# Projections from rows that are not yet normed, in a two-layer hybrid encoder

## What is computed

```python
h = rms_norm(x, norm1_g[i])          # x * rsqrt(mean(x^2) + 1e-6) * g, per token
proj = h @ w_in[i]
q, k, v, z, xbc, dt_raw, gate_a, gate_m = jnp.split(proj, SPLITS, axis=-1)
q = rms_norm(q.reshape(b, s, 8, 2, 64), qk_norm_g[i, 0])   # per head of 64
k = rms_norm(k.reshape(b, s, 8, 2, 64), qk_norm_g[i, 1])
...
u = silu(conv(xbc, width 5, along the tokens) + conv_b)
dt = softplus(dt_raw + dt_bias);  y = y * silu(z)
```

## Time and profile before

| | us |
|---|---|
| median of three runs | 1734.61 |
| the profiled execution, its own time | 1734.33 |
| its span, first to last instruction | 1732.5 |
| TensorE busy in the span | 1686.1 |
| VectorE, ScalarE, GpSimd busy | 718.0, 683.6, 667.9 |

### The profile page before, as it was taken

How to read it: one execution, slowest core, us unless ns; L and a number is a source line. 1 busy time by engine, 2 the same in 40 slices (tenths; PEclk the granted TensorE clock), 3 DMA queues, 4 the chain that set the end, 5 groups by cost and what they waited for, 6 DMA issues and landing times.

```text
span 1732.5 us, 23236 instructions
## 1 busy us (share of the span) xinstructions
PE 1686.1 (97%) x8975; PEld 1046.0 (60%) x8975; DVE 718.0 (41%) x1351; ACT 683.6 (39%) x1549; POOL 667.9 (39%) x536
## 2 busy tenths in 40 slices
PE   8999999999999999999899999999999999999997
PEld 6889877787434444343378898777874344444342
DVE  6728788524222222221176287875242222122121
ACT  5565787754211111111156557877541111111111
POOL 7788776895000000000077987768940000000000
PEclk9999999999999999999999999999999999999999
DMA  7454312766999999999954452227589999999997
GB/s 285 184 195 152 141 50 102 284 265 275 408 428 428 427 428 427 426 428 428 424 212 162 179 195 98 84 106 283 233 320 414 427 428 427 427 428 428 426 427 311
DMA packets 44659, 528.47 MB, mean 305 GB/s; under 512 B 4824, under 2 KB 7640, under 8 KB 12288
## 3 DMA queue, kind: packets, MB, share of 16 engines
q1 hardware_dynamic: 44512, 526.89, 74.1%
q0 software_dynamic: 32, 0.02, 0.0%
HBM read 525.82 MB, written 1.06 MB: 304 GB/s over the span
## 4 chain that ended last, share of the span: by engine, by line
PE 70%; DMA 13%; DVE 9%; ACT 5%; issue 2%; POOL 1%; SPq 0%; DVEq 0%; ACTq 0%
PE PS L1286 19%; DMA view<-in_w_exp_up_dram 12%; PE PS L1317 11%; PE PS L870 8%; PE PS L872 8%; PE PS L871 8%; DVE view L1987 5%; PE PS L1232 3%; PE PS L1218 2%; DVE view L1983 1%; PE PS L1077 1%; PE PS L1219 1%; ACT view L1555 1%; DMA wr<-in_w_router_dram 1%; PE PS L858 1%
## 5 line engine op out<-in xcount | busy, mean ns | idle before, releaser
L2368 POOL TENSOR_TENSOR view<-view,view 128x512 fp32r<-128x512 f32 x448 | 579.8, 1317 | 543.2 <-ACT view L1441 532.4
L1286 PE MATMUL PS<-view,view 128*64 128x512 f32 x2044 | 455.4, 595 | 19.2 <-DMA view<-in_w_exp_gate_dram 9.9
L1441 ACT ACTIVATE view<-view 128x512 fp32r<-128x512 f32 x448 | 274.5, 631 | 150.7 <-PE PS L872 147.7
L1286 PEld LDWEIGHTS PS<-view,view 128*64 128x64 f32 x2044 | 143.1, 137 | 301.3 <-issue 263.5
L870 PE MATMUL PS<-view,view 128*128 128x512 f32 x704 | 285.4, 405 | 5.1 <-POOL view L2368 3.2
L872 PE MATMUL PS<-view,view 128*128 128x512 f32 x704 | 275.1, 391 | 0.0
L871 PE MATMUL PS<-view,view 128*128 128x512 f32 x704 | 274.9, 391 | 0.0
L2268 DVE SCALAR_TENSOR_TENSOR view<-PS,gcol,view 128x512 fp32r<-128x512 f32 x64 | 48.0, 751 | 476.3 <-ACT view L1754 459.0
L1317 PE MATMUL PS<-view,stb 128*64 128x512 f32 x1024 | 227.7, 596 | 4.4 <-ACT stb L1730 1.5
L1317 PEld LDWEIGHTS PS<-view,stb 128*64 128x64 f32 x1024 | 70.3, 137 | 137.3 <-issue 125.6
L870 PEld LDWEIGHTS PS<-view,view 128*128 128x128 f32 x704 | 132.5, 188 | 32.6 <-issue 5.1
(11 more groups left out here) (263 smaller groups left out, 2028.1 us busy)
## 6 DMA issues: line engine op xcount, KB each, us to landing
view<-in_w_exp_up_dram SPq DMA_DIRECT2D x60, 2048.0 KB, 26.9
view<-in_w_exp_gate_dram SPq DMA_DIRECT2D x60, 2048.0 KB, 26.9
view<-in_w_mix_dram SPq DMA_DIRECT2D x54, 2048.0 KB, 7.6
...
view<-in_w_mix_dram SPq DMA_DIRECT2D x8, 512.0 KB, 17.9
...
```

Of the source, the lines that this page charges most:

```text
L1286: ins = pe.matmul(bank(ph, name, j)[e * CAP:(e + 1) * CAP, :], xgT1[:, k, at + e * CAP:at + (e + 1) * CAP], weight_rows(j, kind, row, 1), ...
L1441: nc.scalar.activation(highs(chunk), weights(slot8, chunk), ACT.Copy).then_inc(*high_ready.up(ph))
L2368: g_.tensor_tensor(weights(low8, chunk), weights(slot8, chunk), highs(chunk), ALU.subtract).then_inc(*low_ready.up(ph))
```

## The change

The transposes take X itself; hTh and hTl hold rows that are not normed. ScalarE's squares move behind the casts of chunks 4 to 7. VectorE turns their sums into a per-token floor that takes the place of epsilon in the four q and k chains (`floor_rows`), computes r after the chain of b = 2 (`norm_rows`), and r is applied to v and z as ScalarE reads them out of PSUM, and to dt. After b = 6 TensorE spreads r over the partitions (two products), and `spread_rows` on VectorE adds the halves, multiplies by r and splits them again into hTh and hTl ahead of the convolution; the first column group there waits for the four pairs (hn_ready). Blocks 1 and 2 of the next layer are issued after the first transposes of that layer are done, and `bridge` is four long instead of seven. At the start of the program the first quarter of block 0 is loaded ahead of the table's inputs, VectorE writes the ones first, TensorE runs ten filler products at once, the product of the table stands behind four transposes, and two fillers follow it. GpSimd's low halves no longer wait for the normed rows.

The diff, cut to what acts on the order of work:

```diff
         if b == 5:
             f += [(("ac",), 5)]
+        if b == 6:
...
         ybuf = view(slot_at[5] + 3072, 2, COLS)
         hTh = view(r_h, KD, TT * P, dt=F32R)
-        XN = view(r_xn, TT, D)
...
         bc_dt, bc_al, bc_d, bc_rb = (bc[:, a:b] for a, b in ((0, o_al), (o_al, o_d), (o_d, o_rb), (o_rb, o_lq)))
         bc_lq = bc[:, o_lq:].rearrange("p (a b) -> p a b", b=HD)
-        st = sb("stat", [P, 96])
+        st = sb("stat", [P, 98])
         small = sb("small", [P, 48])
...
+            for part in range(EARLY):
+                cols = slice(part * SLOT // QUARTERS, (part + 1) * SLOT // QUARTERS)
+                sp.dma_start(slot8[0].rearrange("p k c -> p (k c)")[:, cols],
+                             w_mix[ds(0, 1)].rearrange("a p f -> p (a f)")[:, cols]).then_inc(*first_loaded[part].up(Phase(0)))
...
-                for part in range(QUARTERS):
+                for part in range(0 if l else EARLY, QUARTERS):
...
+                        if l and i == 1:
+                            sp.wait_ge(*full(ph, "hT", 0))
...
+            pe.wait_ge(s_constv, 2)
+
+            def warm(count):
+
+                for _ in range(count):
+                    pe.matmul(PS[:, 2, :], onesb[:, :], onesb[:, :].unsqueeze(1).to_broadcast([P, 4, P]),
+                              start=True, stop=True, skip_group_check=True)
+
+            warm(10)
             for b in range(8):
                 pe.sem_inc(filled[b].sem, 1)
                 for i in range(DEPTH):
                     pe.sem_inc(over_filled[i][b].sem, 1)
             pe.wait_ge(s_pool, POOL_CONSTS)
-            pe.wait_ge(s_constv, 2)
-            pe.wait_ge(s_rel, 32)
-            pe.matmul(PS[0:HEADS, 7, :], rel[:, :], oh.rearrange("p a b -> p (a b)"),
-                      start=True, stop=True).then_inc(s_tab, 1)
...
-                if l == 0:
-                    keep_busy(5)
-                    pe.wait_ge(s_tabc, 1)
                 def row_turn(k):
 
-                    pe.wait_ge(*xn_ready.at(ph, 4 if k >= KD // 2 else 2))
-                    transpose2(ph, lambda t: XN[:, t, k * P:(k + 1) * P], ("hT", k))
+                    for t in range(TT):
+                        if l:
+                            pe.wait_ge(*out_of(Phase(l - 1), "s", ALL_PAIRS - 1, t, k // (KD // 2)))
+                        else:
+                            pe.wait_ge(s_x[t], 16)
+                    transpose2(ph, lambda t: X[:, t, k * P:(k + 1) * P], ("hT", k))
...
+                if l == 0:
+                    pe.wait_ge(s_rel, 32)
+                    pe.matmul(PS[0:HEADS, 3, :], rel[:, :], oh.rearrange("p a b -> p (a b)"),
+                              start=True, stop=True).then_inc(s_tab, 1)
+                    warm(2)
...
+                    if l == 0 and b == 1:
+                        pe.wait_ge(s_tabc, 1)
...
+                    if b == 6:
+                        pe.wait_ge(*row_ready.at(ph, 1))
+                        pe.wait_ge(*free(ph, "spread"))
+                        for t in range(TT):
+                            ins = pe.matmul(bank(ph, "spread")[:, t * P:(t + 1) * P], r_tok[t].to_broadcast([P, P]),
+                                            ident[:, :], start=True, stop=True)
+                        ins.then_inc(*fill(ph, "spread"))
...
+                                if c == 0 and k % 2 == 0:
+                                    pe.wait_ge(*hn_ready.at(ph, k // 2 + 1))
...
-                    bridge(7)
+                    bridge(4)
...
-                if l:
-                    cast(ph, 0, 2)
-                for i in range(2 * TT):
-                    t, n = divmod(i, 2) if l == 0 else (i % 2, i // 2)
-                    if l:
-                        act.wait_ge(*out_of(Phase(l - 1), "s", ALL_PAIRS - 1, t, n))
-                    else:
-                        act.wait_ge(s_x[t], 16)
-                    nc.scalar.activation(sq[:, (2 * n + t) * COLS:(2 * n + t + 1) * COLS], X[:, t, n * COLS:(n + 1) * COLS],
-                                         ACT.Square, accum_out=small[:, 2 * n + t:2 * n + t + 1]).then_inc(*sumsq.up(ph))
-                if l == 0:
-                    act.wait_ge(s_tab, 1)
-                    nc.scalar.activation(rtab.rearrange("p a b -> p (a b)"), PS[0:HEADS, 7, :], ACT.Copy
-                                         ).then_inc(s_tabc, 1)
-                cast(ph, 2 if l else 0, HIGHS - (2 if l else 0))
+                cast(ph, 0, HIGHS if l else 2)
                 act.wait_ge(*columns_in.at(ph, 1))
                 for k in range(KD):
                     high_of(ph, hTh[:, k, :], ("hT", k), vcol[:, G1 + k:G1 + k + 1])
+                    if l == 0 and k == 1:
+                        cast(ph, 2, 2)
+                    if l == 0 and k == 3:
+                        act.wait_ge(s_tab, 1)
+                        nc.scalar.activation(rtab.rearrange("p a b -> p (a b)"), PS[0:HEADS, 3, :], ACT.Copy
+                                             ).then_inc(s_tabc, 1)
                     if k >= KD // 2:
-                        cast(ph, HIGHS + k - KD // 2, 1)
+                        i = k - KD // 2
+                        cast(ph, HIGHS + i, 1)
+                        t, n = i % 2, i // 2
+                        if l:
+                            act.wait_ge(*out_of(Phase(l - 1), "s", ALL_PAIRS - 1, t, n))
+                        else:
+                            act.wait_ge(s_x[t], 16)
+                        nc.scalar.activation(sq[:, i * COLS:(i + 1) * COLS], X[:, t, n * COLS:(n + 1) * COLS],
+                                             ACT.Square, accum_out=small[:, i:i + 1]).then_inc(*sumsq.up(ph))
...
-                                act.wait_ge(*rs_in.at(ph, 1 + b))
+                                act.wait_ge(*rs_in.at(ph, b))
...
-                            nc.scalar.activation(V[:, t, 0:COLS], bank(ph, "p", b, t), ACT.Copy
+                            act.wait_ge(*row_ready.at(ph, 1))
+                            nc.scalar.activation(V[:, t, 0:COLS], bank(ph, "p", b, t), ACT.Copy, scale=r_tok[t]
...
-                                                 ACT.Silu).then_inc(*drain(ph, "p", b, t))
+                                                 ACT.Silu, scale=r_tok[t]).then_inc(*drain(ph, "p", b, t))
...
+            v.memset(ones[:, :], 1.0).then_inc(s_constv, 1)
+            v.memset(onesb[:, :], 1.0).then_inc(s_constv, 1)
             for b in range(8):
                 dve.sem_inc(drained[b].sem, 1)
                 for i in range(DEPTH):
                     dve.sem_inc(over_drained[i][b].sem, 1)
-            v.memset(ones[:, :], 1.0).then_inc(s_constv, 1)
-            v.memset(onesb[:, :], 1.0).then_inc(s_constv, 1)
...
+                    if floor is None:
+                        v.tensor_scalar(var, var, 1.0 / width, EPS, ALU.mult, ALU.add).then_inc(*rs_in.up(ph))
+                    else:
+                        v.scalar_tensor_tensor(out=var, in0=var, scalar=1.0 / width, in1=floor,
+                                               op0=ALU.mult, op1=ALU.add).then_inc(*rs_in.up(ph))
...
-                def norm_rows():
+                def floor_rows():
 
                     dve.wait_ge(*sumsq.at(ph, 4))
                     link(v.tensor_tensor(st[:, 0:TT], small[:, 0:TT], small[:, TT:2 * TT], ALU.add))
-                    r = rsqrt(TT, 1, D)
-                    for n in range(2):
-                        for t in range(TT):
-                            v.tensor_scalar(XN[:, t, n * COLS:(n + 1) * COLS], X[:, t, n * COLS:(n + 1) * COLS], r[:, t:t + 1],
-                                            None, ALU.mult).then_inc(*xn_ready.up(ph))
-
+                    each(lambda t: v.tensor_scalar(floors[:, 8 * t:8 * t + 8], st[:, t:t + 1].to_broadcast([P, 8]),
+                                                   EPS / D, EPS * EPS, ALU.mult, ALU.add))
+
+                def norm_rows():
+
+                    link(v.tensor_tensor(st[:, 0:TT], small[:, 0:TT], small[:, TT:2 * TT], ALU.add))
+                    r = rsqrt(TT, 4, D)
+                    v.tensor_copy(st[:, 96:96 + TT], r).then_inc(*row_ready.up(ph))
+                    dve.wait_ge(*row_ready.made(ph))
+
+                def spread_rows():
+
+                    halves = [slice(h * KD // 2, (h + 1) * KD // 2) for h in range(2)]
+                    for h in halves:
+                        link(v.tensor_tensor(hN[:, h, :], hTh[:, h, :], hTl[:, h, :], ALU.add))
+                    dve.wait_ge(*full(ph, "spread"))
+                    by_row = bank(ph, "spread")[:, 0:TT * P].unsqueeze(1).to_broadcast([P, KD // 2, TT * P])
+                    link(v.tensor_tensor(hN[:, halves[0], :], hN[:, halves[0], :], by_row, ALU.mult))
+                    v.tensor_tensor(hN[:, halves[1], :], hN[:, halves[1], :], by_row, ALU.mult).then_inc(*drain(ph, "spread"))
+                    dve.wait_ge(*out_of(ph, "spread"))
+                    for i in range(KD // 2):
+                        ks = slice(2 * i, 2 * i + 2)
```

(31 more changed lines are left out.)

15 lines of the change are left out of this document (10 added, 5 removed).

## The result

The changed kernel takes 1743.32 us (median of 6 runs, 1741.12 to 1746.92), the kernel before beside it 1735.3 us (6 runs). The ratio is 1.0045, with a 95% interval of 1.0031 to 1.0060: slower by 0.45%, 7.8 us, where 1731.6 was forecast and 1740.0 was the upper end of the range. The profiled execution took 1744.31 us, its span is 1742.6 us, 10.1 longer than the span of before.

A forecast was written before the change was run, and what follows sets the result against it. TensorE, busy 1686.1 of 1732.5 us, was taken as the bound. From the profiled 1734.33 us, -2.8 - 1.9 + 1.0 + 0.4 + 0.6 = -2.7 gave 1731.6 us, with eight in ten from 1727.5 to 1740.0.

The forecast's parts named there:

- Layer 1's start, -2.8: Between the layers: the norm leaves the path, four fillers remain, the first transposes start 2.8 us earlier.
- The two loads, 0: Issuing layer 1's blocks 1 and 2 later costs and gains nothing; bounds +1.5 and -1 us.
- Layer 0's start, -1.9: First product comes 3.1 us earlier, but TensorE waits 1.8 for the first q chain: 1.9 us gained, bounds -3.8 to 0.
- norm_rows, 0: On VectorE ahead of block 3's reduces: 13 small instructions, 9.2 us, just fit into idle time and slack, costing nothing.
- The rival in which it is late: norm_rows between blocks 2 and 3 outlasts 9.6 us and delays TensorE: 1738.4 or 1745.0 us; chance 0.14.
- Spread products, +1.0: TensorE's two added products per layer cost 0.5 us per layer, 1.0 in all.
- Split, +0.2 per layer: VectorE's copies and subtractions before the convolution: only the last pair cannot be early, 0.2 us per layer (0 to 0.5).
- GpSimd, +0.3 per layer: GpSimd may lose time to VectorE's four long and eight short instructions: 0.3 us per layer (0 to 2.5).
- The port rival: VectorE's new work holds up GpSimd through shared SBUF ports, 2.5 us per layer: 1736.0 us; chance 0.06.
- TensorE idle under 0.5 us in the first convolution group: A sign named for the profile after: TensorE hardly waits at the start of the convolution.
- the two signs that I named for a wrong prediction: TensorE waits for VectorE ahead of block 3's transposes, or the cast of chunk 8 waits for a load.
- five cases: Forecast 0.50, more gain kept 0.20, first q chain sets both starts 0.10, norm_rows late 0.14, ports 0.06.

The follow-up runs named there:

- e11: e8 with seven filler products instead of four between the layers: 1737.67 us, ratio 1.0012.
- e9: e8 with two filler products instead of four between the layers: 1734.33 us, ratio 0.9990.
- e10: e8 without the wait that holds blocks 1 and 2 of the second layer behind its first transposes: 1738.11 us, ratio 1.0020.
- f4: e8 with more filler products at the program's start, and without the wait ahead of layer 1's blocks 1 and 2: 1736.69 us, ratio 1.0015.
- e4: The changed kernel without the wait that holds blocks 1 and 2 of the next layer behind its first transposes: 1741.61 us, ratio 1.0033.
- e1: The changed kernel with ScalarE copying the split's high halves, VectorE only subtracting: 1736.46 us, ratio 1.0000.
- e13: The changed kernel with column and shared vectors loaded ahead of block 1, without the rescaling's sums, multiplications and split: 1732.63 us, ratio 0.9984.
- e8: The changed kernel with ScalarE copying the split's high halves and the column and shared vectors loaded ahead of block 1: 1733.7 us, ratio 0.9993.
- e12: The kernel before the change, with only the column and shared vectors loaded ahead of block 1: 1735.0 us, ratio 0.9997.

## Why the prediction was wrong, step by step

- **Layer 1's start, -2.8**: the number is right, 876.98 against the last down products gives -2.87; the mechanism only in part. More fillers do delay the transposes (e11), but fewer do not bring them forward (e9): four happened to end when the other thing that holds TensorE did, and that was luck. And without the deferral the transposes start 2.2 to 2.5 us later.
- **The two loads, 0**: the number held for the casts, which never waited for block 1. The mechanism failed. I asked only who waits for the deferred load and whether the last expert loads would come sooner; I did not ask what else the traffic holds up. Without the deferral 2.2 to 2.5 us of the 2.8 above are lost (e10, f4, e4). The sum had that gain right, but put it down to the fillers alone; a reader who had dropped the deferral as worthless on my word would have lost it.
- **Layer 0's start, -1.9**: half right. Links and wait came as drawn (first product at 9.94 for 10.6 to 10.8, wait 1.88 for 1.8), the transposes at 36.44 for 35.6, as TensorE arrived at 34.56 for 33.7 and the chain ended later by as much. The chain also had a second cause that the prediction put at nothing: `floor_rows`, with its sum 4.0 us in after where at most 3 x 1.22 was allowed. The step that failed is that a wait costs its own length. Behind it the clock was at half for over 3 us, and of -1.0 nothing was left at 52.8 us.
- **norm_rows, 0**: right. Its 13 instructions took 8.4 us in layer 0 and 7.9 in layer 1 for 9.2 estimated, and no transposes waited for them. The rival in which it is late did not come.
- **Spread products, +1.0**: about right, 0.36 us for the two of a layer, 0.7 in all.
- **Split, +0.2 per layer**: the step that failed and broke the forecast. I wrote that only the last pair cannot be early, and gave that pair 2.6 us beside a busy GpSimd; I did not apply the 2.6 to the other three. At 3.16 us a pair (the free price was put at 1.1) four pairs need 12.65 us, and block 8 leaves some 8 from the place where the first may be written. So it is the duration of an instruction beside GpSimd, times eight; the earlier trace rows warned of it, with small links at 1.22 us for 0.17. With two waits of 2.06 and the clock behind them the term is 3.9 us a layer instead of 0.2 (e1: 7.8 for both, from medians).
- **GpSimd, +0.3 per layer**: the four long instructions were priced at 1.28 each, from rows with no GpSimd beside them. The sums took 2.25. The term is near 1.1 in layer 0 and 0.6 in layer 1 (e13); together with the spread products it is 1.3 us a layer, in layer 1 as 111.73 - 110.41 and in layer 0 as 87.08 - 85.76 (e8 less e12).
- **The port rival** had the right mechanism and the wrong victim. By the Trainium skill, SBUF — State Buffer, "SBUF: two separate sides", a VectorE operation with two SBUF inputs and a GpSimd operation exclude each other, and the prediction turned that against GpSimd. The trace agrees with the page (2.25 against 1.22 us for the same size with one operand in PSUM), but the loser that mattered was VectorE, with TensorE behind it. The copies of the split, with one SBUF input, took 1.51 to 1.59 us there too; no run has one without GpSimd beside it.
- **What would show it**: I named "TensorE idle under 0.5 us in the first convolution group" as a sign. It was 2.06 us, in both layers, and is the first row of the waits that is new. Neither of the two signs that I named for a wrong prediction came: TensorE did not wait ahead of the transposes of block 3, and chunk 8's cast did not wait for a load. They stood at the steps that I doubted, not at the one that failed.

With these terms repaired (the clock behind the q wait, the split, and GpSimd together with the spread products) the sum comes out: 1734.3 - 2.9 - 1.0 + 1.5 (clock behind the q wait: from 36.44 to 52.8, -1.0 turns to +0.5) + 7.8 + 2 x 1.3 = 1742.3, beside 1744.31 in the profiled execution. The 7.8 is the measured difference to e1 and no estimate of its own, so this is a tally and not a test. The remaining 2 us are not traced to a place; the last stretch, from the convolution of layer 1 on, varies by 1.5 to 2.8 by itself.

None of the five cases had the late split, and the ones above 1736.0 rested on norm_rows, which was on time. The range was too narrow because the split was bounded at 0.5 us a layer from one pair, instead of at four pairs beside GpSimd, and because no case had a wait with the clock at half behind it.
